# Final sums of a hybrid encoder layer: ten tiles spread over TensorE, GpSimd and VectorE, second rows loaded from two queues

## What is computed

```python
xn2 = rmsnorm(x, norm2_g[l])
x = x + hier_moe(xn2, ...)          # top-1 group of 4, top-2 experts of 8 inside it
...
hb = silu(matmul(xb, w_gate[eb])) * matmul(xb, w_up[eb])
y = matmul(hb, w_down[eb])          # summed over a token's two experts, each with its weight
...
return rmsnorm(x, final_norm_g)     # x * rsqrt(mean(x * x) + 1e-6) * final_norm_g
```

## Time and profile before

| what | us |
|---|---|
| median of 3 runs (lowest, highest) | 1166.03 (1163.17, 1167.06) |
| profiled execution, its own time | 1163.27 |
| span of that execution in the trace | 1161.5 |
| busy in the span: TensorE, VectorE, ScalarE, GpSimd | 1139.5, 862.1, 688.6, 258.1 |

### The profile page before, as it was taken

How to read it: one execution, slowest core, us unless ns; L and a number is a source line. 1 busy time by engine, 2 the same in 40 slices (tenths; PEclk the granted TensorE clock), 3 DMA queues, 4 the chain that set the end, 5 groups by cost and what they waited for, 6 DMA issues and landing times.

```text
span 1161.5 us, 18098 instructions
## 1 busy us (share of the span) xinstructions
PE 1139.5 (98%) x5934; PEld 961.9 (83%) x5934; DVE 862.1 (74%) x1343; ACT 688.6 (59%) x1134; POOL 258.1 (22%) x345
## 2 busy tenths in 40 slices
PE   7999999999999999999999999999999999999997
PEld 7988888888889988887788888888888888888873
DVE  6649510124547866667899999999999999999997
ACT  6342241223337744335687887877878878878754
POOL 2200210001200012223232323323323223233240
PEclk9999989999999999999999999999999999999999
DMA  7312240436969744453999999999999999999989
GB/s 226 88 37 83 91 137 1 128 126 208 308 239 375 248 146 145 146 200 123 402 383 390 392 393 398 385 399 390 388 399 379 391 394 386 396 390 382 396 315 356
DMA packets 110146, 324.09 MB, mean 279 GB/s; under 512 B 22454, under 2 KB 59232, under 8 KB 85520
## 3 DMA queue, kind: packets, MB, share of 16 engines
q1 hardware_dynamic: 93104, 281.79, 65.5%
q0 software_dynamic: 16992, 41.64, 9.3%
HBM read 285.37 MB, written 51.12 MB: 290 GB/s over the span
## 4 chain that ended last, share of the span: by engine, by line
PE 91%; DMA 4%; DVE 3%; ACT 1%; issue 1%; SPq 0%; POOL 0%; ACTq 0%; DVEq 0%; POOLq 0%
PE psum L953 26%; PE psum L955 25%; PE psum L954 25%; PE psum L1237 2%; PE psum L1272 1%; PE psum L1143 1%; PE psum L1078 1%; PE psum L1079 1%; PE psum L1319 1%; PE psum L1311 1%; PE psum L1086 1%; PE psum L1298 1%; DMA units<-mlstm_units 1%; PE psum L1124 1%; PE psum L999 1%
## 5 line engine op out<-in xcount | busy, mean ns | idle before, releaser
L2057 DVE TENSOR_TENSOR e_lo<-e_st,e_hi 128x1024 fp32r<-128x1024 f32 x384 | 447.0, 1224 | 10.6 <-ACT e_hi L1553 10.6
L1553 ACT ACTIVATE e_hi<-e_st 128x1024 fp32r<-128x1024 f32 x384 | 375.8, 1052 | 9.9 <-DMA e_st<-in_expert_w_gate_dram 4.2
L953 PE MATMUL psum<-e_hi,ex_hi 128*128 128x512 f32 x512 | 199.4, 389 | 0.1
L955 PE MATMUL psum<-e_hi,ex_lo 128*128 128x512 f32 x512 | 199.5, 390 | 0.0
L954 PE MATMUL psum<-e_lo,ex_hi 128*128 128x512 f32 x512 | 199.2, 389 | 0.0
L953 PE MATMUL psum<-xT_hi,w_hi 128*128 128x512 f32 (+1 forms) x432 | 151.5, 351 | 2.2 <-DVE w_lo L1693 1.4
L955 PE MATMUL psum<-xT_hi,w_lo 128*128 128x512 f32 (+1 forms) x432 | 149.4, 346 | 0.0
L954 PE MATMUL psum<-xT_lo,w_hi 128*128 128x512 f32 (+1 forms) x432 | 149.4, 346 | 0.0
L953 PEld LDWEIGHTS psum<-e_hi,ex_hi 128*128 128x128 f32 x512 | 96.1, 188 | 20.5 <-issue 0.3
L955 PEld LDWEIGHTS psum<-e_hi,ex_lo 128*128 128x128 f32 x512 | 96.1, 188 | 20.0
L954 PEld LDWEIGHTS psum<-e_lo,ex_hi 128*128 128x128 f32 x512 | 96.1, 188 | 19.9
(11 more groups left out here) (292 smaller groups left out, 1859.8 us busy)
## 6 DMA issues: line engine op xcount, KB each, us to landing
e_st<-in_expert_w_gate_dram SPq DMA_DIRECT2D x64, 1024.0 KB, 8.4
e_st<-in_expert_w_up_dram SPq DMA_DIRECT2D x64, 1024.0 KB, 9.7
e_st<-in_expert_w_down_dram SPq DMA_DIRECT2D x64, 1024.0 KB, 11.0
mlstm_units<-stage SPq DMA_DIRECT2D x18, 640.0 KB, 4.0
w_st<-in_w_in_dram SPq DMA_DIRECT2D x20, 512.0 KB, 4.4
xn_scratch<-xn POOLq DMA_DIRECT2D x20, 512.0 KB, 3.9
e_st<-expert_rows SPq DMA_DIRECT2D x20, 512.0 KB, 7.7
stage<-gate_rows SPq DMA_DIRECT2D x18, 512.0 KB, 6.1
```

The lines of the kernel that those rows point to most:

```text
L953: pe.matmul(out, a_hi, b_hi, start=start, stop=False)
L955: return pe.matmul(out, a_lo, b_hi, start=False, stop=stop)
L1553: act.activation(e_hi[:, r, :, :], e_st[:, slot, :, :], ACT.Copy).then_inc(ehi_done, 1)
L2057: dve.tensor_tensor(e_lo[:, r, :, :], e_st[:, slot, :, :], e_hi[:, r, :, :].bitcast(F32), ALU.subtract).then_inc(elo_done, 1)
```

## The change

The ten late sums are dealt anew: TensorE takes tiles 1, 3, 6 and 7, GpSimd 2, 5 and 8, VectorE 0, 4 and 9. GpSimd also takes a third early sum, tile 2. The early loads come in the order 0, 3, 1, 6, 2, 7, 4, 5, 8, 9. TensorE writes all four first parts ahead of all four second parts, and the waits for a norm are gone. VectorE adds tile 4 ahead of its norm of tile 2, and tile 9 ahead of that of tile 7. Every second late load is issued by ScalarE, ahead of its squares. The core of the diff:

```diff
-    ON_POOL = (0, 1)
+    EARLY_ORDER = (0, 3, 1, 6, 2, 7, 4, 5, 8, 9)
+    EARLY_POOL = (0, 1, 2)
+    EARLY_DVE = (3, 6, 7, 4, 5, 8, 9)
+    LATE_ORDER = (0, 2, 1, 3, 5, 4, 6, 8, 7, 9)
+    ON_PE = (1, 3, 6, 7)
+    LATE_POOL = (2, 5, 8)
+    LATE_DVE = (0, 4, 9)
...
-        return t % 8
+        return EARLY_ORDER.index(t) % 8
...
-    ON_PE = (2, 4, 5, 7, 8, 9)
-    LATE_ORDER = (0, 2, 1, 3, 4, 5, 6, 7, 8, 9)
...
+        def late_load(eng, t):
+            slot = late_slot(t)
+            if slot < 8:
+                wait_early_sum(eng, EARLY_ORDER[slot])
+            eng.dma_start(spare(slot), y_dram[T + t * P:T + (t + 1) * P, :]).then_inc(e_load[slot], 16)
...
-            for t in LATE_ORDER:
-                slot = late_slot(t)
-                if slot < 8:
-                    wait_early_sum(sp, slot)
-                sp.dma_start(spare(slot), y_dram[T + t * P:T + (t + 1) * P, :]).then_inc(e_load[slot], 16)
+            for t in LATE_ORDER[0::2]:
+                late_load(sp, t)
...
+            for t in LATE_POOL:
+                wait_early_sum(pool, t)
+                add_rows(t, late_slot(t), late_loads(t, 2 * n_half - 1))
...
             keep_warm_late(24)
-            for j in range(3):
-                if j:
+            for j in range(len(ON_PE)):
+                if 0 < j < 3:
                     keep_warm_late(8)
                 first_row_part(j)
             for j in range(len(ON_PE)):
-                if j >= 4:
-                    pe.wait_ge(f_done, ON_PE[j - 4] + 1)
-                if j >= 3:
-                    first_row_part(j)
                 second_row_part(j)
...
+            for b in range(2):
+                act.wait_ge(y_out[b], 16 * n_half)
+            for t in LATE_ORDER[1::2]:
+                late_load(act, t)
             for t in range(NT):
-                if t in ON_PE:
...
+                wait_sum(act, t)
...
-            early_sum(2)
+            early_sum(EARLY_DVE[0])
             y_half(last_i, 1, last_piece(last_i, 3)[0] + 1, bank=0)
-            for t in range(3, NT):
+            for t in EARLY_DVE[1:]:
                 early_sum(t)
-            for t in range(NT + 2):
-                if t < NT and t not in ON_PE:
-                    late_sum(t)
-                if t >= 2:
-                    final_norm(t - 2)
+            late_ahead = {0: 0, 2: 4, 7: 9}
+            for t in range(NT):
+                if t in late_ahead:
+                    late_sum(late_ahead[t])
+                final_norm(t)
```

More of the change, by code:

```diff
@@ L230, in build @@
     gf_b = at("gf_b", ROWS + 4 * KB, [P, D], F32)
-    ON_POOL = (0, 1)
+    EARLY_ORDER = (0, 3, 1, 6, 2, 7, 4, 5, 8, 9)
[5 more added lines that the diff above has]
+    LATE_DVE = (0, 4, 9)
+    LAST_ROUTED, LAST_OUT = 2, 0
     def spare(slot):
@@ L237, in early_slot @@
     def early_slot(t):
-        return t % 8
+        return EARLY_ORDER.index(t) % 8
     def late_slot(t):
         return 2 + LATE_ORDER.index(t)
-    LAST_ROUTED, LAST_OUT = 2, 0
-    ON_PE = (2, 4, 5, 7, 8, 9)
-    LATE_ORDER = (0, 2, 1, 3, 4, 5, 6, 7, 8, 9)
     psum = nc.alloc_psum_tensor("psum", [P, 8, 512], F32)
@@ L482, in early_loads @@
         def early_loads(t, last):
-            return row_loads(early_slot(t), 1 if t < 8 else 2, last)
+            return row_loads(early_slot(t), EARLY_ORDER.index(t) // 8 + 1, last)
         def late_loads(t, last):
@@ L490, in wait_early_sum, with wait_sum @@
         def wait_early_sum(eng, t):
-            if t in ON_POOL:
-                eng.wait_ge(f_pool, ON_POOL.index(t) + 1)
-            else:
-                eng.wait_ge(f_sum, t + 1 - len(ON_POOL))
-        def sums_taken(t):
-            return NT - len(ON_POOL) + sum(x not in ON_PE for x in range(t + 1))
+            if t in EARLY_POOL:
+                eng.wait_ge(f_pool, EARLY_POOL.index(t) + 1)
+            else:
+                eng.wait_ge(f_sum, EARLY_DVE.index(t) + 1)
+        def wait_sum(eng, t):
+            if t in ON_PE:
+                eng.wait_ge(f_pe_sum, ON_PE.index(t) + 1)
+            elif t in LATE_POOL:
+                eng.wait_ge(f_pool, len(EARLY_POOL) + LATE_POOL.index(t) + 1)
+            else:
+                eng.wait_ge(f_sum, len(EARLY_DVE) + LATE_DVE.index(t) + 1)
+        def late_load(eng, t):
[3 more added lines that the diff above has]
+            eng.dma_start(spare(slot), y_dram[T + t * P:T + (t + 1) * P, :]).then_inc(e_load[slot], 16)
         def pe_sum(t):
-            return two((2, 4, 0, 6)[ON_PE.index(t) % 4])
+            return two((2, 4, 0, 6)[ON_PE.index(t)])
         def load_half_steps(eng):
@@ L743, in _ @@
             sp.dma_start(gf_b[:, :], final_norm_g.rearrange("(a d) -> a d", a=1).broadcast_to([P, D])).then_inc(norms_in, 16)
-            for t in range(NT):
+            for n, t in enumerate(EARLY_ORDER):
                 slot = early_slot(t)
-                if t == 0:
+                if n == 0:
                     sp.wait_ge(elo_done, gu_piece(last, 7)[0] + 1)
-                elif t == 4:
+                elif n == 4:
                     sp.wait_ge(elo_done, down_piece(last, 3)[0] + 1)
-                elif t >= 8:
-                    wait_early_sum(sp, t - 8)
+                elif n >= 8:
+                    wait_early_sum(sp, EARLY_ORDER[n - 8])
                 sp.dma_start(spare(slot), y_dram[t * P:(t + 1) * P, :]).then_inc(e_load[slot], 16)
@@ L890, in weights_in, with add_rows @@
                     bounds_check=2 * T - 1, oob_is_err=False).then_inc(factor_in[b], 16)
-            def early_sum(t, last):
-                slot = early_slot(t)
-                pool.wait_ge(e_load[slot], early_loads(t, last))
+            def add_rows(t, slot, loads):
+                pool.wait_ge(e_load[slot], loads)
                 pool.sem_inc(pool_past, 1)
@@ L935, in _ @@
             pool.sem_inc(pool_past, 1)
-            for t in ON_POOL:
-                early_sum(t, 2 * n_half - 1)
+            for t in EARLY_POOL:
+                add_rows(t, early_slot(t), early_loads(t, 2 * n_half - 1))
             for b in range(2):
@@ L1666, in _ @@
             act.activation(wts[:, 3, 0:1], epsc[:, :], ACT.Sqrt)
+            for b in range(2):
+                act.wait_ge(y_out[b], 16 * n_half)
+            for t in LATE_ORDER[1::2]:
+                late_load(act, t)
             for t in range(NT):
-                if t in ON_PE:
[L1669 to L1673, removed]
+                wait_sum(act, t)
+                total = pe_sum(t) if t in ON_PE else x1[:, t, :].rearrange("p (a n) -> p a n", a=2)
                 if t >= 1:
```

## The result

| | median, us | executions | ratio to before, 95% interval |
|---|---|---|---|
| before | 1164.65 | 14 | |
| changed | 1168.01 | 14 | 1.0033 [1.0024, 1.0042] |

The account below looks back on a forecast made before the run. TensorE's order bounded the tail; delays of 1.83 and 1.72 us, then VectorE's closing row, moved its end from 1158.45 to 1161.64, +3.19 us: on the median 1166.03, 1169.2 us, range 1164.6 to 1172.4.

Parts of the forecast that it names:

- Third early sum holds the third low part, +1.83: At VectorE's last low parts: GpSimd's third early sum comes in first, so TensorE's last unread matmuls start 1.83 us later.
- Rival 1: At the low parts: GpSimd does not get in ahead of the third, so +1.36 us, 1167.4; chance 0.21.
- TensorE's order, +1.72: In TensorE's late sums: tile 7's first part stands ahead of the first complete sum, now tile 1's, delaying it 1.72 us.
- VectorE becomes the bound: Behind tile 1's scaling, from 1146.98: VectorE's eight norms and two late sums set the end, 1161.64 against 1158.45 before.
- rival 3: At the tail's end: TensorE's 6.9 us saved, with 1.83 lost, reach the end, giving 1161.0 us; chance 0.08.
- Late sums on GpSimd: Before VectorE's late sum of tile 4: GpSimd's three late sums end by 1148 and cost nothing, by 0.2 us.
- Rival 2: In VectorE's closing row: GpSimd's addition of tile 8 holds tile 4's late sum, 0.7 to 2.14 us more; chance 0.29.
- Two queues: At the late loads: the eighth lands 12.45 to 13.8 us after the first issue; neither moves the sum.
- Early sums on VectorE: Ahead of tile 0's late sum: seven instead of eight, some 1.1 us less, covered by VectorE's wait for tile 1.

Follow-up runs that it names:

- the fourth first part back: Changed kernel with TensorE's fourth first part (tile 7) behind tile 1's second part instead of ahead of it: 1167.45 us, 1.0017 of before.
- one queue: Changed kernel with all ten late loads issued by SP: 1168.89 us, 1.0032 of before.
- the run with the first rows on it: Changed kernel without GpSimd additions, TensorE adding first rows of tiles 1, 3, 6, 7 in place of unread products, ten first-row slots: 1162.11 us, 0.9991 of before.

## Why the prediction was right

- **Third early sum holds the third low part, +1.83.** Right: 3.40 us by the chain. TensorE's first unread matmul came 12.20 - 10.28 = 1.92 later behind the transposes (1125.63 - 1115.35 = 10.28 before), and 1.75 of tail came back when the sum was moved to VectorE. Writing alone, GpSimd held nothing. Rival 1 falls. That the third low part is the one held was in part luck: with the fourth first part back, and with one queue, it was not, and TensorE still began as late (11.91 and 11.94).
- **TensorE's order, +1.72.** Right in size: tile 1's sum is complete at 1147.01, 30.03 behind the transposes; the first one before was 1141.73 - 1115.35 = 26.38. That is +3.65 for the 1.83 and 1.72 together, so 1.73 for the order. Undoing the order alone gave back only 1.1 of it, as a load was then late.
- **VectorE becomes the bound.** Right: from the scaling of tile 1 at 1148.71 it has no idle time. That start was forecast at 1146.98, and is 1148.71 - 1.63 = 1147.08 when the transposes' shift is taken off. TensorE's 6.9 us of saved time stood behind this point and were worth nothing, so rival 3 falls.
- **Late sums on GpSimd, "I count nothing for it, by 0.2 us".** This term was mis-sized: 0.89. Rival 2 named the mechanism and gave 0.7 to 2.14, and by the prediction's own sign for it (a late sum of 2 to 3.4 us beside GpSimd's addition) it came true with 2.11, on top of the forecast and not in its place. GpSimd's addition of tile 8 began 1.65 us later than forecast, against a margin of 0.2: the first late load went out 0.9 later than forecast (tile 9's first rows ran beside the last scatter, a moved DMA that I had not followed), the eighth load landed 13.0 us after the first issue, between the two bounds, where I took 12.45, and GpSimd started 0.17 behind the landing. These steps add up, but the first is not shown to be a cause: with tile 9's load back in its place the loads went out 0.95 earlier and GpSimd started 0.17 earlier.
- **Two queues.** "Neither moves the sum" holds for the kernel before (no change in its row). In the changed kernel it hides a part of GpSimd's hold: 0.91 of tail between one queue and two.
- **Early sums on VectorE.** Covered, as forecast: VectorE waited 3.94 us for tile 1.

So the forecast's mechanism held up to VectorE's closing row, and there rival 2's hold came on top. By the tail the forecast lacked 1.0 us of the 4.21. That the medians' +3.4 lies so near to its +3.2 is luck, since the interval, 2.8 to 4.9 us, would have held either; that its median, 1169.2, lies above the 1168.01 has to do with its base, the three runs' 1166.03, which lay 1.4 above the later median of the kernel before.

## What to carry to other kernels

When tiles pass through engines in order, look for the first tile behind which one engine has no idle time. In this tail that engine's row alone set the time from there on: TensorE's 6.9 us saved behind that tile were worth nothing, and the parts added ahead of it were paid in full. An addition given to GpSimd is not free for VectorE: each meeting cost it up to 2.1 us here, against 1.13 for doing the sum itself. Where such a helper is taken away, see also to what its work released (slots, loads), and try to fill an engine's waits with its own later products before adding an engine.

## What the runs showed of the hardware that was not expected

- The turns alternate over a whole row: in the changed kernel three sums of GpSimd (9.55 us) and three low parts (8.41) interleave one by one, so one held addition makes the next GpSimd one longer too (3.37, where one alone took 2.35). The Trainium skill (SBUF — State Buffer, "Who interferes with whom") says that the issue order decides which engine blocks. The rows agree, and show that the waiting engine comes next.
- The hold falls on VectorE's scalings too: 3.18 and 3.19 us in place of 1.28 with both input tiles in SBUF, but 1.28 beside the same addition with one in PSUM. A write of 512 KB by GpSimd (0.95 us) held nothing; the same section says so.
- TensorE kept the higher of its two clocks (granted 1.00 from 1126 to 1152 us) in the run with the first rows on it, with waits of 1.92, 0.59 and 0.58 us and no unread matmuls.
